# Matrix products of constant tables ahead of the norm waits, and the residual row products between the column sums

## What is computed

```
mod = silu(c) @ w_mod[l] + b_mod[l]                  # six rows of 1024
sh_a, sc_a, g_a, sh_f, sc_f, g_f = split(mod, 6)
h = rms_norm(x, norm_mix[l]) * (1 + sc_a) + sh_a
x = x + g_a * (mixer(h @ w_in[l]) @ w_out[l])
h = rms_norm(x, norm_ffn[l]) * (1 + sc_f) + sh_f
x = x + g_f * ((silu(h @ w_gate[l]) * (h @ w_up[l])) @ w_down[l])
```

```
x = x + head_group_mixer(rmsnorm(x, mix_norm[l]), ...)
x = x + memory_cross_attn(rmsnorm(x, xa_norm[l]), rmsnorm(mem, mem_norm[l]), ...)
x = x + peer_ffn(rmsnorm(x, peer_norm[l]), ...)
```

## Time and profile before

| | |
|---|---|
| runs | 2905.5, 2906.28, 2903.01 us; median 2905.5 |
| the profiled execution's own time | 2902.05 us |
| its span, first to last instruction | 2900.3 us |
| PE busy | 2791.4 us, 96% of the span |
| PEld, DVE, ACT, POOL busy | 2382.6, 2090.9, 1408.0, 192.0 us |
| mean granted TensorE clock | 0.98 of 2.4 GHz |
| read from HBM | 527.48 MB, 184 GB/s over the span |

### The profile page before, as it was taken

One profiled execution on the slowest core, in us unless ns is written; L12 is line 12 of the kernel. 1 busy time (PEld: TensorE's weight loads), 2 busy tenths in 40 slices (PEclk: granted clock), 3 DMA queues, 4 the chain that ended last, 5 costly groups with the idle time before them and its releaser, 6 DMA issues. The chain is left out here.

```text
span 2900.3 us, 40006 instructions
## 1 busy us (share of the span) xinstructions
PE 2791.4 (96%) x16468; PEld 2382.6 (82%) x16468; DVE 2090.9 (72%) x3086; ACT 1408.0 (49%) x1620; POOL 192.0 (7%) x168
## 2 busy tenths in 40 slices
PE   6989999999999999999999999998999999999998
PEld 6768888788888788888878888887888888888887
DVE  6777866665543669989879955435599989699755
ACT  4554445554456445554444444484445544444443
POOL 0200001000003001110000000030011200000000
PEclk9989999999999999999999999999999999999999
DMA  8747854545543355554445555533445544455554
GB/s 320 288 174 272 311 206 168 202 167 192 192 180 131 117 174 175 189 174 162 173 160 189 175 189 195 217 126 121 157 163 189 189 160 163 158 192 174 186 193 148
DMA packets 75637, 537.41 MB, mean 185 GB/s; under 512 B 8512, under 2 KB 8896, under 8 KB 12096
## 3 DMA queue, kind: packets, MB, share of 16 engines
q1 hardware_dynamic: 75456, 534.86, 52.7%
HBM read 527.48 MB, written 7.34 MB: 184 GB/s over the span
## 5 line engine op out<-in xcount | busy, mean ns | idle before, releaser
L946 ACT ACTIVATE whi<-raw 128x2048 fp32r<-128x2048 f32 x438 | 838.6, 1915 | 985.9 <-issue 827.6
L1396 DVE TENSOR_TENSOR wlo<-raw,whi 128x2048 fp32r<-128x2048 f32 x438 | 1006.3, 2298 | 331.0 <-ACT whi L946 330.3
L428 PE MATMUL banks<-ht,whi 128*128 128x512 f32 x3136 | 771.5, 395 | 7.4 <-DVE big L1470 5.4
L428 PEld LDWEIGHTS banks<-ht,whi 128*128 128x128 f32 x3136 | 576.5, 189 | 123.3 <-issue 6.9
L503 PE MATMUL banks<-whi,ht 128*128 128x512 f32 x1152 | 459.6, 399 | 18.2 <-DVE ht L1460 10.0
L505 PE MATMUL banks<-whi,ht 128*128 128x512 f32 x1152 | 452.7, 393 | 0.0
L436 PEld LDWEIGHTS banks<-ht,wlo 128*128 128x128 f32 x3136 | 401.9, 191 | 15.8
L436 PE MATMUL banks<-ht,wlo 128*128 128x256 f32 x3136 | 406.6, 283 | 0.0
L513 PE MATMUL banks<-wlo,ht 128*128 128x512 f32 x1152 | 287.4, 389 | 0.0
L503 PEld LDWEIGHTS banks<-whi,ht 128*128 128x128 f32 x1152 | 218.6, 190 | 65.3 <-issue 19.3
L505 PEld LDWEIGHTS banks<-whi,ht 128*128 128x128 f32 x1152 | 218.7, 190 | 44.3
(11 more groups left out here) (259 smaller groups left out, 3263.6 us busy)
## 6 DMA issues: line engine op xcount, KB each, us to landing
raw<-in_pu SPq DMA_DIRECT2D x128, 1024.0 KB, 4.9
raw<-in_pv SPq DMA_DIRECT2D x128, 1024.0 KB, 4.9
raw<-in_win SPq DMA_DIRECT2D x52, 1024.0 KB, 4.9
big<-in_wmod SPq DMA_DIRECT2D x24, 1024.0 KB, 6.4
raw<-in_wmod SPq DMA_DIRECT2D x24, 1024.0 KB, 4.9
raw<-in_wgate SPq DMA_DIRECT2D x22, 1024.0 KB, 4.9
raw<-in_wup SPq DMA_DIRECT2D x22, 1024.0 KB, 4.9
raw<-in_wdown SPq DMA_DIRECT2D x22, 1024.0 KB, 4.9
```

The source lines that it names most:

```text
L428: m = e.matmul(bank[b + n], h[:, q, c[n]], M.both[:, q * 512:(q + 1) * 512], start=q == 0, stop=False, skip_group_check=True)
L946: e.activation(whi(j), slot[u][0], ACT.Copy).then_inc(*hi.mark(j))
L1396: e.tensor_tensor(wlo(j), slot[u][0], whi(j).bitcast(F32), ALU.subtract).then_inc(*lo.mark(j))
```

## The change

A function `warm` is added to PE's list. It takes bank 7 and multiplies the identity with `SM[:, 0:256]` n times into it, a 128x256 fp32 product each; nothing reads the result. It stands ahead of `turn_all` at the start (n = 7), at mix2 (9 for l = 0, 6 for l = 1), at x (6) and at peer (6). At the three boundaries with a modulation, the two products of the gate row move from behind `turn_all` into the column sums, one ahead of the sixth and one ahead of the twelfth of the 16. The gate row of mix1(0) stays where it was.

```diff
+        def warm(name, n, b=7):
+            clear(("warm", *name), b)
+            on.wait_ge(*d_const.at(0))
+            for _ in range(n):
+                e.matmul(bank[b][:, 0:256], IDN, SM[:, 0:256], start=True, stop=True)
+
-        def modulation(l, part, b=None):
+        def modulation(l, part, b=None, between=None):
...
             for q in range(16):
+                if between is not None and q in (5, 11):
+                    between(q // 11)
                 m = e.matmul(bank[b][:, q:q + 1], sums[q], ONES[:, 0:1], start=True, stop=True)
             m.then_inc(*modsum.mark((l, part)))
 
-        def gate_row(l, g, bs=(None, None)):
+        def gate_row(l, g, bs=(None, None), part=(0, 1)):
             on.wait_ge(*mac.at((l, 1 + g, 7)))
-            for q in range(2):
+            for q in part:
...
             if l == 0:
+                warm(name, 7)
                 turn_all(("m", 0), MEM, DG[1])
...
             else:
-                modulation(1, 0)
+                modulation(1, 0, None, lambda q: gate_row(1, 0, (0, 1), (q,)))
                 turn_all(name, XA, DG[0])
-                gate_row(1, 0, (0, 1))
...
         def feed_forward(l):
             name = ("ffn", l)
-            modulation(l, 1)
+            modulation(l, 1, None, lambda q: gate_row(l, 1, (0, 1), (q,)))
             turn_all(name, XA, DG[0])
-            gate_row(l, 1, (0, 1))
...
         def second_mixer(l):
             name = ("mix2", l)
+            warm(name, 6 if l else 9)
             turn_all(name, XA, DG[0])
...
         def cross(l):
             name = ("x", l)
+            warm(name, 6)
             turn_all(name, XA, DG[0])
...
         def peer(l):
             name = ("peer", l)
+            warm(name, 6)
             turn_all(name, XA, DG[0])
```

## The result

The changed kernel took **2893.74 us** (median of 8 runs, 2890.36 to 2897.6) beside 2903.09 for the kernel before (8 runs, 2901.22 to 2906.28): ratio 0.9968, 95% interval 0.9957 to 0.9979. Of the 7.1 us between the forecast 2900.8 and the measured time, 2.4 come from the starting point: the forecast was counted from 2905.5, the median of three runs of the kernel before, which over eight runs is 2903.09. The profiled execution took 2894.23 us, span 2892.5.

A forecast was written before the change was run, and what follows sets the result against it. PE, busy 96% of the span, was taken as the bound, at whatever clock it gets. Fills -9.1, ffn gate rows +4.4, mix1(1) and start 0 gave -4.7 us: 2900.8 from a 2905.5 median, range 2895.5 to 2906.5.

The forecast's parts named there:

- The fill at mix2, x and peer, -9.1: At mix2, x and peer: filling PE's idle gap before turn_all holds the clock, regaining five boundaries' 9.07 us; ends 0 and -9.1.
- The gate rows at ffn, +4.4: At ffn(0) and ffn(1): gate rows among the sums delay diag, +2.2 us each, +4.4 together.
- The sum's own bounds: At ffn: +0.77 (ffn(0)) and +0.54 (ffn(1)) with the clock held; +4.4 at the very worst for ffn(0).
- the middle at ffn(0): At ffn(0): +2.2 us, taken between +0.8 and +3.6, leaving out the very worst end.
- the gate row's old place is worth nothing in ffn: At ffn, behind turn_all: the row ran while PE would have waited anyway; PE still waited 0.30 us after it.
- mix1(1), "I take 0": At mix1(1): slack and the returned 1.7 us offset the late chain; 0, ends -1.2 (clock held) and +1.7 (lost).
- the step's best end: At mix1(1): -1.2 us with the clock held, the first unit running to 446.3.
- mix1(0) and the start, 0: At the start: second key unit waits for weights until 25.68, so the fill gains 0, between -0.5 and +1 us.
- (a): Rival, at the sums: gate rows do keep the clock, total -9.0 us, 2896.5; chance 0.25.
- (b): Rival: fill does not hold the clock, or its gain is lost inside stages; 2909.9 at most, 2905 with half kept; chance 0.10.
- (c): Rival, at the fills: the fill itself runs at half clock and delays the turns, 2924 us; chance 0.05.

## Why the forecast missed

**The fill at mix2, x and peer, -9.1.** The mechanism and the boundary's size were right. In all fourteen profiled executions with full fills all six boundaries took 6.16 us, 84 of 84; the five without fills there lost 8.97 to 9.21 us. Here the Trainium skill ("TensorE: Matmul & The Clock Gate", Part 4: PE-mode transpose) had been weighed against the trace. Its rule that transposes do not count for the clock would have made the term 0; the runs show that it does not reach to plain products with an identity. The term's size was short, since it counted the boundaries only. Those six stages together are 11.6 us shorter over the fourteen executions than over the five, and 12.5 shorter in the kernel with the fills alone than in the kernel before (table): 2.5 to 3.4 us more. Over the fourteen and the five it lies in the two mix2 stages, which are 5.6 us shorter together, 3.0 of it at their boundaries. The two places just shown are where: the first lost the clock in three of ten mix2 stages without fills and in both with small fills, in none of 28 with full ones; the second in all ten and both, and in 17 of the 28. So what failed in this term is that it ended at the last remainder. Why the later places are spared stays open: that PE leaves the boundary earlier and at full clock fits, and was not tested by itself.

**The gate rows at ffn, +4.4.** Right in size and way, in part by luck. The two stages cost +5.1 in three executions each; over all executions with the rows between the sums and `columns` in its place (five, against thirteen with the rows behind the turn) +2.4 and +2.0. The sum's own bounds hold: 3.13 us more until `columns` at ffn(0), 1.62 at ffn(1), as forecast between 1.70 or 1.47 and 4.35. But the middle at ffn(0) stands for no execution: where the clock held among the sums (three of the five) the stage took 196.6 to 196.7 us, 0.7 to 0.8 more than the 195.9 of the kernel before, and where it was lost (two) 200.3 to 200.4, 4.4 to 4.5 more. One reading of the sum was wrong: that the gate row's old place is worth nothing in ffn. With the rows there the clock never fell behind the turn (26 ffn stages); with the rows moved it fell there in 6 of 14, the two with everything at full clock up to the turn among them. By runs, moving the ffn rows back gave 3.6 us (means 2893.8 and 2890.1, without the start's fill) and 7.5 (2894.1 and 2886.7, with it). The chain through DVE is how the first microseconds arise, but not what sets the price: with diag ahead of `columns` nothing came back.

**mix1(1), "I take 0": the step that failed.** It measured -2.4 in three executions each, and over all executions 191.02 us with the rows between the sums (13, at most 191.93) against 193.26 with the rows behind the turn (6, at least 192.38): -2.2. Outside its ends of -1.2 and +1.7, too. Until `columns` it cost the +0.82 that was forecast (436.87 - 431.49 = 5.38, against 4.51 and the step to DVE). But the turn held the clock, the first unit began 441.71 - 431.49 = 10.22 us after the first sum against 440.82 - 428.57 = 12.25, and the second at 447.85, 16.36 after it. Before, it began at 446.70, 18.13 after it: 1.77 came back, where the step's best end was 1.2 (it had the first unit end at 446.3). That is the case of five of the thirteen. In three (the third execution of the changed kernel among them) the clock fell behind the sums, the turn took 6.6 to 6.8 us and the second unit began 18.1 to 18.3 us after the first sum, so the boundary gave nothing; yet the stage was as short, 190.9 to 191.0, since a later place, 54 us into the stage, where both other executions of the changed kernel lost the clock, was spared. By whole runs the move at mix1(1) gave 3.4 us with the start's fill (means 2890.0 and 2886.7) and 0.5 without it (2890.6 and 2890.1), so the stage shows it better than the total does. The step erred in choosing the middle between held and lost, and in ending its account at the boundary.

**mix1(0) and the start, 0.** mix1(0) is 2.1 us shorter in the table, but it scatters by 11 us over the twenty profiled executions, and over all of them it is 2.7 us shorter with the start's fill (12 against 8; standard error 1.1). The runs do not settle it, as said above.

**The rivals.** (a) gave nearly the right sum, -9.0, by the wrong way: it has the rows at ffn cost 1.3 us, and they cost 4 to 5. (b) is ruled out by 84 of 84 and by stages that gained more than the boundaries, (c) by 2.75 us for twelve instructions. That the forecast -4.7 fell short by 4.65 is thus, in the table's terms: mix1(1) -2.4, mix1(0) -2.1, the fill's stages -10.4 in place of -9.1, ffn +5.1 in place of +4.4; these give -5.1, and the three executions differ by 10.1 us where the medians differ by 9.35. By whole runs the miss lies in two parts: the fills alone gave -12.1 in place of -9.1, and the gate rows alone +2.1 in place of +4.4, a difference of about what mix1(1) gave. (The range's high end should read 2906.3 by its own sum, +0.8 on 2905.5.)

**A version that beats both** leaves the gate rows behind the turn at ffn and moves them at mix1(1) only: 2884.4, 2884.9 and 2886.6 us in three sets of runs, 7 us under the changed kernel and 16 under the kernel before. That `columns` behind diag on top gives another microsecond or two is not shown: the intervals overlap.

## What to carry to other kernels

When an engine must wait for a short chain, harmless work in the gap can buy the clock of what follows, but it has to fill the gap: with a third of it four of six boundaries still lost the clock. Work put among cheap instructions that something waits for is paid at once, and at which boundary it pays is to be measured one by one: here the same edit gave 2 us at one place and cost 4 to 5 at two others together, and both hid in one sum. Work that seems to fill only a wait may be holding the clock there, as the gate rows in their old place did. Price a change of clock over the whole stage, since the places at which PE is thin inside it shift with it.

## What the runs showed of the hardware

Matmuls of one column need not hold the clock though PE counts as busy: after 3.63 us of such sums at ffn(0), with PE busy throughout, the granted clock fell from 1.00 to 0.54, and four rows took 3.50 us; at ffn(1), in the same execution, the same sums were followed by the same rows in 1.96 us. And the clock is lost at the same places inside a stage, by execution or not: 3.3 us at a time in mix2(0) and in mix2(1). The Trainium skill ("TensorE: Matmul & The Clock Gate", Part 1) calls the number of slow matmuls while the clock comes up variable from run to run, and that penalty under 1% of a typical span, not to be fitted. The trace agrees that it varies; the loss at the six boundaries, 9.1 us, is 0.3% of this span, about the whole of what the change gains. The losses of a whole run are more: a mean granted clock of 0.98 puts them at up to 2% of the span (an estimate).
